# Winograd pairs in the second half of the third projections of a two-block transformer kernel

## What is computed

```python
h = rms_norm(x, norm_g[l])
proj = h @ w_in[l]
(aq, ak, av, az, iq, ik, iw, bcq, bckv, bkpe, bz, cq, cz, gates) = jnp.split(proj, IN_OFFSETS, axis=-1)
...
o_c = memory_attention(cq, ck, cv).reshape(bsz, seq, C_WIDTH)
u = jnp.stack([o_a * jax.nn.silu(az), o_b * jax.nn.silu(bz), o_c * jax.nn.silu(cz)], axis=2)
```

## Time and profile before

| | us |
|---|---|
| median of three runs | 2404.72 |
| the profiled execution | 2404.98 |
| its span, first to last instruction | 2403.2 |
| TensorE busy | 2396.6 |
| VectorE busy | 1852.0 |
| ScalarE busy | 1233.5 |
| GpSimd busy | 321.2 |

### The profile page before, as it was taken

One profiled execution on the slowest core, in us unless ns is written; L12 is line 12 of the kernel. 1 busy time (PEld: TensorE's weight loads), 2 busy tenths in 40 slices (PEclk: granted clock), 3 DMA queues, 4 the chain that ended last, 5 costly groups with the idle time before them and its releaser, 6 DMA issues.

```text
span 2403.2 us, 34102 instructions
## 1 busy us (share of the span) xinstructions
PE 2396.6 (100%) x10809; PEld 1981.8 (82%) x10809; DVE 1852.0 (77%) x2664; ACT 1233.5 (51%) x1582; POOL 321.2 (13%) x277
## 2 busy tenths in 40 slices
PE   9999999999999999999999999999999999999999
PEld 7888888888888888888888888888888888888887
DVE  5467679897888988988888897668867876587584
ACT  5445455555455444444444455455557555555443
POOL 0021242234210000000000000011101000521050
PEclk9999999999999999999999999999999999999999
DMA  7555555576655655555555556955554545544654
GB/s 272 192 186 178 179 178 175 183 245 228 226 186 184 202 197 193 190 194 189 189 199 194 194 190 210 253 185 177 184 190 163 180 166 182 177 167 167 227 193 166
DMA packets 134827, 464.25 MB, mean 193 GB/s; under 512 B 14544, under 2 KB 21328, under 8 KB 134112
## 3 DMA queue, kind: packets, MB, share of 16 engines
q1 hardware_dynamic: 122464, 443.08, 54.4%
q10 hardware_dynamic: 12256, 20.15, 2.7%
q0 software_dynamic: 32, 0.03, 0.0%
HBM read 455.87 MB, written 7.34 MB: 193 GB/s over the span
## 4 chain that ended last, share of the span: by engine, by line
PE 96%; DVE 2%; issue 1%; ACT 1%; DVEq 0%; ACTq 0%
PE PS L682 21%; PE PS L684 21%; PE PS L683 21%; PE PS L931 7%; PE PS L929 7%; PE PS L930 7%; PE PS L949 3%; PE PS L950 3%; PE PS L951 3%; DVE WL L1727 1%; DVE PT L1843 1%; PE PS L798 1%; PE PS L767 1%; PE PS L723 0%; PE PS L1108 0%
## 5 line engine op out<-in xcount | busy, mean ns | idle before, releaser
L1169 ACT ACTIVATE WH<-RAW 128x1024 fp32r<-128x1024 f32 x841 | 888.3, 1059 | 1083.4 <-PE PS L684 684.0
L1727 DVE TENSOR_TENSOR WL<-RAW,WH 128x1024 fp32r<-128x1024 f32 x811 | 1021.0, 1268 | 470.3 <-ACT WH L1169 460.0
L682 PE MATMUL PS<-WH,HT 128*128 128x512 f32 (+1 forms) x1816 | 715.7, 394 | 0.3 <-DVE WL L1727 0.2
L684 PE MATMUL PS<-WH,HT 128*128 128x512 f32 (+1 forms) x1816 | 706.1, 389 | 0.0
L683 PE MATMUL PS<-WL,HT 128*128 128x512 f32 (+1 forms) x1816 | 705.4, 388 | 0.0
L682 PEld LDWEIGHTS PS<-WH,HT 128*128 128x128 f32 x1816 | 341.1, 188 | 71.8 <-issue 3.7
L684 PEld LDWEIGHTS PS<-WH,HT 128*128 128x128 f32 x1816 | 340.9, 188 | 71.0
L683 PEld LDWEIGHTS PS<-WL,HT 128*128 128x128 f32 x1816 | 341.2, 188 | 67.9
L929 PE MATMUL PS<-WH,HT 128*128 128x512 f32 x704 | 274.0, 389 | 0.0
L931 PE MATMUL PS<-WH,HT 128*128 128x512 f32 x704 | 273.9, 389 | 0.0
L930 PE MATMUL PS<-WL,HT 128*128 128x512 f32 x704 | 273.9, 389 | 0.0
(11 more groups left out here) (320 smaller groups left out, 2338.5 us busy)
## 6 DMA issues: line engine op xcount, KB each, us to landing
RAW<-w_stream SPq DMA_DIRECT2D x841, 512.0 KB, 3.4
bias_scratch<-BE ACTq DMA_DIRECT2D x12, 256.0 KB, 4.0
MEMR<-mem_in ACTq DMA_DIRECT2D x1, 2048.0 KB, 10.7
X<-x_in ACTq DMA_DIRECT2D x4, 512.0 KB, 5.1
x_scratch<-X ACTq DMA_DIRECT2D x4, 512.0 KB, 5.1
X<-x_scratch ACTq DMA_DIRECT2D x1, 2048.0 KB, 11.2
out<-X ACTq DMA_DIRECT2D x8, 256.0 KB, 3.1
X<-x_in SPq DMA_DIRECT2D x3, 512.0 KB, 9.3
```

Source lines behind the costliest of these rows:

```text
L682: pe.matmul(o, hi, WH[:, slot, kk, 0:cols], start=k == 0, stop=False)
L684: ins = pe.matmul(o, lo, WH[:, slot, kk, 0:cols], start=False, stop=k == nq * GK - 1)
L1169: act.activation(WH[:, g.slot(j)], RAW[:, g.slot(j)], ACT.Copy).then_inc(hi_split, 1)
L1727: dve.tensor_tensor(WL[:, s], RAW[:, s], WH[:, s].bitcast(F32), ALU.subtract).then_inc(lo_split, 1)
```

## The change

The second half of `c_proj` (groups 16 to 31, product chunks 2 and 3) becomes one product of 2x2 blocks. The rows of `h` split in halves (t = 0, 1), the columns in chunks 2 and 3, and the inner dimension in eight pairs of 128-feature tiles, q = 0 to 7. The stream is read in another order, so that groups 2i and 2i+1 are both chunks for the same q, with q in the order 4, 0, 5, 1, 6, 2, 7, 3.

For q = 0 to 3 (`eight`) the pair is done as before with eight block products. For q = 4 to 7 (`seven`) it is done with Winograd's seven block products M1 to M7. Their left sums S1 to S4 are made once by GpSimd from `HROWS`, which VectorE now scales by the gains at steps 0 to 3; ScalarE and VectorE split them at steps 9 and 10. Their right sums are made for each pair s = 0 to 3 from the group slots a and b: GpSimd makes T3 = B22-B12 into `TX`, then T1 = B12-B11 in place in `RAW` of b, then T2 = B22-T1; VectorE makes B21-T2. ScalarE's split of b waits for T1. ScalarE splits three sums (`TXH`), VectorE their low parts (`TXL`) behind the next group's split. `TX` and its split parts have two buffers. The products run in the order M1, M2, M5, M3, M6, M7, M4; M6 waits for `tx_lo`. The load that takes the slots of a and b waits for `tx_made`. All eight banks hold sums; at the end ScalarE copies one and VectorE adds the parts together into `PB`, seven additions from PSUM, in place of ScalarE's two copies.

```diff
         HROWS = sb("HROWS", [P, KT // 2, S], F32, at_pa + 24 * KB)
+        HBLK = HROWS[:].rearrange("p (q e) (t s) -> p q e t s", e=2, t=T)
+        TX = [sb(f"TX{n}", [P, 3, CH], F32, at) for n, at in enumerate((at_pa, at_pa + 24 * KB))]
+        SUMH = sb("SUMH", [P, 4, 4, P], F32R, at_pa + 8 * KB)
+        SUML = sb("SUML", [P, 4, 4, P], F32R, at_pa + 16 * KB)
+        SUMR = sb("SUMR", [P, 4, 4, P], F32, at_u0)
+        TXH = sb("TXH", [P, 2, 3, CH], F32R, at_x)
+        TXL = sb("TXL", [P, 2, 3, CH], F32R, at_u0)
+        ZU = [sb(f"ZU{n}", [P, CH], F32, at) for n, at in enumerate((at_x + 12 * KB, at_x + 14 * KB, at_pa + 32 * KB, at_pa + 34 * KB))]
         MEMT = sb("MEMT", [P, KT, 2, S], F32R, at_pb)
         MEMX = sb("MEMX", [P, KT, S], F32, at_pa)
         MQKV = sb("MQKV", [P, T, 3 * W], F32, at_pb)
@@ -329,6 +337,18 @@
         x_loaded = sem("x_loaded")
         mem_turned = sem("mem_turned")
...
+        M1, M2, M3, M4, M5, M6, M7, C22 = range(8)
+        own = 2 * (PROD0["c_proj"] % 2)
+        other = 2 - own
+        BANK = {M1: 4, M2: 5, M5: 6, M3: 7, M6: own, M7: own + 1, M4: other, C22: other + 1}
+        HALFWAY = 2 * GD
+        PAIR_Q = (4, 0, 5, 1, 6, 2, 7, 3)
+
+        def seven_of(j):
+
+            i = (j - HALFWAY) // 2
+            return i // 2 if 0 <= i < GD and i % 2 == 0 else None
...
-            with sp.Fori(1, GROUPS // RING) as r:
-                for s in range(RING):
-                    sp.wait_ge(lo_split, r * RING + (s + 1 - RING))
-                    load(None, ds(r * RING + s, 1), s)
+            paired = GROUP0["c_proj"] + HALFWAY
+            assert paired % RING == 0
+
+            def rounds(first, last):
+                with sp.Fori(first // RING, last // RING) as r:
+                    for s in range(RING):
+                        sp.wait_ge(lo_split, r * RING + (s + 1 - RING))
+                        load(None, ds(r * RING + s, 1), s)
+            rounds(RING, paired)
+            for j in range(2 * GD):
+                s = seven_of(HALFWAY + j - RING)
+                if s is not None:
+                    sp.wait_ge(tx_made, s + 1)
+                sp.wait_ge(lo_split, paired + j + 1 - RING)
+                load(None, ds(paired + j % 2 * GD + PAIR_Q[j // 2], 1), j % RING)
+            sp.wait_ge(tx_made, GD // 2)
+            rounds(paired + 2 * GD, GROUPS // RING * RING)
...
+            hold(rows_scaled, 1)
+            a11, a12, a21, a22 = [HBLK[:, :, e, t, :] for t in range(T) for e in range(2)]
+            s1, s2, s3, s4 = [SUMR[:, n] for n in range(4)]
+            link(pool.tensor_tensor(s1, a21, a22, ALU.add))
+            link(pool.tensor_tensor(s2, s1, a11, ALU.subtract))
+            link(pool.tensor_tensor(s3, a11, a21, ALU.subtract))
+            pool.tensor_tensor(s4, a12, s2, ALU.subtract).then_inc(sums_made, 1)
+            hold(sums_made, 1)
+            for s in range(GD // 2):
+                g, j = At(GROUP0["c_proj"]), HALFWAY + 4 * s
+                a, b = g.slot(j), g.slot(j + 1)
+                hold(raw_landed[a], g.turn(j) * 16 + 16)
+                hold(raw_landed[b], g.turn(j + 1) * 16 + 16)
+                if s >= 2:
+                    hold(tx_lo, s - 1)
+                b11, b12, b22 = RAW[:, a, 0], RAW[:, b, 0], RAW[:, b, 1]
+                link(pool.tensor_tensor(TX[s % 2][:, 2], b22, b12, ALU.subtract))
+                pool.tensor_tensor(b12, b12, b11, ALU.subtract).then_inc(t1_made, 1)
+                hold(t1_made, s + 1)
+                pool.tensor_tensor(TX[s % 2][:, 0], b22, b12, ALU.subtract).then_inc(t2_made, 1)
...
             products("c_proj", [(GD, HT)] * 2, 0, None, h3_rest)
-            product_loop("c_proj", 2, [(GD, HT)] * 2, first=1)
+
+            gc, nc0 = At(GROUP0["c_proj"]), PROD0["c_proj"]
+
+            def block_products(o, left, wide, start, stop):
+                (hi, lo), (bh, bl) = left, wide
+                pe.matmul(o, hi, bh, start=start, stop=False)
+                pe.matmul(o, hi, bl, start=False, stop=False)
+                return pe.matmul(o, lo, bh, start=False, stop=stop)
+
+            def tile(k, t):
+                cols = slice(t * P, (t + 1) * P)
+                return HT[:, k, 0, cols], HT[:, k, 1, cols]
+
+            def eight(q, j, first, last):
+
+                for c, outs in enumerate(((M2, M4), (M3, C22))):
+                    def body(slot):
+                        for kk in range(GK):
+                            for t in range(T):
+                                ins = block_products(PS[:, BANK[outs[t]], :], tile(q * GK + kk, t), (WH[:, slot, kk], WL[:, slot, kk]),
+                                                     first and outs[t] == C22 and kk == 0, last and kk == GK - 1)
+                        return ins
+                    group(gc, j + c, body)
+
+            def seven(q, j, s, first, last):
+
+                a, b = gc.slot(j), gc.slot(j + 1)
+
+                def sums(n):
+                    return SUMH[:, n, q - 4, :], SUML[:, n, q - 4, :]
+
+                def wide(slot, kk):
+                    return WH[:, slot, kk], WL[:, slot, kk]
+
+                def extra(n):
+                    return TXH[:, s % 2, n], TXL[:, s % 2, n]
+                k = GK * q
+                parts = {M1: (tile(k, 0), wide(a, 0)), M2: (tile(k + 1, 0), wide(a, 1)), M3: (sums(3), wide(b, 1)),
+                         M4: (tile(k + 1, 1), extra(1)), M5: (sums(0), wide(b, 0)), M6: (sums(1), extra(0)), M7: (sums(2), extra(2))}
+                for m in (M1, M2, M5, M3, M6, M7, M4):
+                    if m == M1:
+                        pe.wait_ge(lo_split, gc.count(j + 1))
+                    if m == M5:
+                        pe.wait_ge(lo_split, gc.count(j + 2))
+                    if m == M6:
+                        pe.wait_ge(tx_lo, s + 1)
+                        if first:
+                            pe.wait_ge(prod_free, nc0 + 3)
+                    if m == M4 and first:
+                        pe.wait_ge(prod_free, nc0 + 4)
+                    ins = block_products(PS[:, BANK[m], :], *parts[m], first, last and m in (M1, M5, M6, M7))
+                    if m in (M2, M3):
+                        ins.then_inc(group_used, 1)
+                    if m == M4:
+                        ins.then_inc(tx_used, 1)
+            pe.wait_ge(sums_lo, 1)
+            for i, q in enumerate(PAIR_Q):
+                j = HALFWAY + 2 * i
+                if i % 2 == 0:
+                    seven(q, j, i // 2, i == 0, i == GD - 2)
+                else:
+                    eight(q, j, i == 1, i == GD - 1)
...
             for p in range(4 * GD):
                 g = At(GROUP0["c_proj"])
+                s = seven_of(p + RING) if p % 2 else None
+                if s is not None:
+                    act.wait_ge(t1_made, s + 1)
                 split(g, p + RING)
                 if p < 3:
                     turned_hi(2, (10 + 2 * p, 11 + 2 * p), "norm2")
-                evacuations("c_proj", g, 0, p, 4, lambda c: PB[:, :, c:c + CH])
+                if p == 9:
+                    act.wait_ge(sums_made, 1)
+                    act.activation(SUMH[:], SUMR[:], ACT.Copy).then_inc(sums_hi, 1)
+                if s is not None:
+                    act.wait_ge(tx_made, s + 1)
+                    if s >= 2:
+                        act.wait_ge(tx_used, s - 1)
+                    act.activation(TXH[:, s % 2], TX[s % 2][:], ACT.Copy).then_inc(tx_hi, 1)
+                if p < HALFWAY:
+                    evacuations("c_proj", g, 0, p, 4, lambda c: PB[:, :, c:c + CH])
+                if p == 4 * GD - 3:
+                    act.wait_ge(tx_used, GD // 2)
+                    act.activation(ZU[0][:], PS[:, BANK[M1], :], ACT.Copy).then_inc(z_copied, 1)
...
+            z, u2, u3, u4 = [part[:] for part in ZU]
+
+            def add(o, m, x):
+                return dve.tensor_tensor(o, PS[:, BANK[m], :], x, ALU.add)
+
+            def c_out(t, c):
+                return PB[:, t, (2 + c) * CH:(3 + c) * CH]
             for p in range(4 * GD):
                 if p < 4:
                     turned_lo("h3", (8 + 2 * p, 9 + 2 * p), "norm2")
+                    for k in (8 + 2 * p, 9 + 2 * p):
+                        o = HROWS[:, k - HALF]
+                        dve.wait_ge(tr_lo, TR["h3"] + k + 1)
+                        ins = dve.tensor_scalar(o, o, par("norm2", k), None, ALU.mult)
+                    if p == 3:
+                        ins.then_inc(rows_scaled, 1)
                 split(At(GROUP0["c_proj"]), p + RING)
+                s = seven_of(p + RING) if p % 2 else None
+                if p == 10:
+                    dve.wait_ge(sums_hi, 1)
+                    dve.tensor_tensor(SUML[:], SUMR[:], SUMH[:].bitcast(F32), ALU.subtract).then_inc(sums_lo, 1)
+                if s is not None:
+                    dve.wait_ge(t2_made, s + 1)
+                    a = At(GROUP0["c_proj"]).slot(p + RING - 1)
```

(26 more changed lines are left out.)

12 lines of the change are left out of this document (added).

## The result

The changed kernel takes 2419.86 us, the median of 2418.0 to 2420.29, beside 2404.76 (2404.53 to 2404.99) for the kernel before: 1.0061 times as long, 95% interval 1.0051 to 1.0071. It is 15.1 us slower where 5.7 were forecast, and lies above the range (2405.0 to 2416.5). The profiled execution took 2419.76.

What follows compares the result with a forecast made beforehand. The prediction took TensorE alone to bound the kernel. Its terms, -2.72 + 4.0 + 4.3 + 0.1 = +5.7 us on the profiled 2404.98, gave 2410.7, or 2410.4 for the median; range 2405.0 to 2416.5.

Steps and rivals of the forecast that it cites:

- Removed: In four c_proj pairs, 21 matmuls in place of 24: 2.72 us saved, all on the bound.
- First pair: TensorE's wait before the first M6 in c_proj: 3.5 us, with 0.5 from upstream 4.0.
- `tx_made` to `tx_lo`: Splitting the right sums on ScalarE, then VectorE's low parts behind the next group's: 5.42 us.
- Landing to `tx_made`: From group b's landing until GpSimd and VectorE have made the right sums: 5.56 us.
- Upstream: VectorE's scalings at steps 1 to 3 and GpSimd's four sums delay loads: 0.5 us, bounds 0 and 2.
- The rings: Later pairs' loops from `tx_made` to `tx_made`: 12.3, 11.3, 11.3 against 10.20 us of TensorE; waits total 4.3 us.
- the latency: Load time of the next a and b: 5.5 us first, 4.5 for the last two; bounds 3.2 and 8.5.
- the meeting: GpSimd's T3 runs beside VectorE's low part of a: 0.75 us more per loop; by the lock 1.4 more in all.
- rival C: Waits near 4 us drop TensorE to the 1.2 GHz level; one return costs 2.2 us: 2412.6; chance 0.15.
- Left sums: ScalarE's and VectorE's splits at steps 9 and 10 lie in leads of over 5 us: nothing.
- The end: Last pair's additions and later Silu use up a_proj's 1.4 us of room: 0.1 us, bounds 0 and 0.5.
- D: Slower parts: GpSimd 1.62 per operation (3.4 us) or first looped load 8.5 (3.0 us); 2413.4 to 2416.8; chance 0.16.

Runs made afterwards that it cites:

- x8: Changed kernel without c_proj's eight bias transfers, bias additions replaced by clears at the start of the next phase's queue; 2412.86 us, ratio 1.0036.
- x2: Changed kernel with T3, T1 and T2 made by VectorE instead of GpSimd, ahead of its low part of b, B21-T2 right behind; 2409.21 us, ratio 1.0021.
- x3: Changed kernel with eighteen extra matmuls, results thrown away, ahead of the first wait before M6; 2422.0 us, ratio 1.0073.
- x7: Changed kernel with only its end mended: bias additions moved to next phase, a_proj's banks freed earlier, Silu and waits reordered; 2417.21 us, ratio 1.0051.
- x0: Changed kernel with M6, M7 and M4 taking split left sums, so TensorE does not wait for `tx_lo`; right sums still made; 2419.51 us, ratio 1.0059.
- x1: Changed kernel with M6, M7 and M4 of the first three pairs put behind the following eight-product pair; 2419.22 us, ratio 1.006.
- x4: Changed kernel without c_proj's eight bias transfers, bias additions replaced by clears in VectorE's steps 26 and 28; 2418.07 us, ratio 1.0055.

## Why the prediction was wrong

The direction and the mechanism were right: late waits before M6 in each pair, ended by `TXL`, and a ring through the loads. The sizes were not, and the clock and the end, which it took as nearly nothing, were not nothing. By its own steps, in us:

- *Removed, 2.72.* Right.
- *First pair, 4.0; it was 4.5.* `tx_made` to `tx_lo`, 5.42, was 5.39. Landing to `tx_made` was 5.96 for 5.56: GpSimd's operation takes 1.28, and half of line 577's 2.41 came out too short (0.17 for the two); VectorE's low part of b took 1.35 for 1.14 beside T2. Upstream was put at 0.5 between 0 and 2. It was 1.0 to 1.1: b landed at 1545.24 for 1544.50, and TensorE was 0.3 earlier. But it did not come the way that I had given, by low parts that delay the load: the load was issued at 1535.55, before at 1535.97, and took 9.6 us for 8.5. What made it longer no run shows. TensorE's restart took back 0.2 (0.06 behind `TXL` for 0.27), and small gaps before M6 another 0.2.
- *The rings, 12.3, 11.3 and 11.3; they were 13.9, 12.7 and 12.7.* This is the step that failed: 4.4 us. The first has the latency 7.5, not 5.5, and no meeting. I had both bounds, and took the lower part although the step before said that two bias transfers would be issued at about the same moment. x8 without them gives 12.7, with the meeting. The others have the meeting: I charged 0.75, one operation of GpSimd against one of VectorE. But VectorE comes to it late, with three low parts back to back, so T1 and T2 meet it too: 7.8 for 5.9 from landing to `tx_made`, 1.9 a ring. Without the meeting these two rings would be 10.8 by the same rows, an estimate. x2, where nothing meets and the sums take 2.9, has 10.45, and there VectorE's queue sets it.
- *The clock (rival C, 0.15).* It happened twice, at 2.5 and 1.7 where one return was priced at 2.2. That it has a rival's name and not a place in the sum is a second miss. What I had missed: a fall inside a ring that binds is free (x3), so the length of the wait is not what prices it, but whether anything behind it can take it up. The one behind the last wait cost 1.7 (nine matmuls in 3.75 us for 2.04).
- *Left sums, nothing.* No wait of TensorE is theirs. Their first operation took 4.38, beside four low parts that took 5.73; whether that has a part in the late landing above is not tested, since no run leaves them out.
- *The end, 0.1, bounds 0 and 0.5; it was 1.8* (2.61 for 0.77 behind c_proj). I had seen that the room of 1.4 us was used up by a Silu 1.4 later, and then charged 0.1. Silu came 4.8 after the last group for the forecast's 3.7, behind pair additions that were late themselves, with two bias additions (1.75 each) ahead of them on VectorE. A spent room is not a price of nothing but one from which every further delay counts in full. x7 takes 1.0 of it; the 0.8 at the head values stays.
- *Overlooked.* The evacuation of chunk 1 stands behind ScalarE's wait for `tx_made`, and its bank is M4's. It costs nothing while M6 is later, but it alone would have kept 1.9 of the wait (x0), and 3.3 of it where TensorE comes earlier (x1).

Together 0.5 + 4.4 + 1.7 + 1.7 = 8.3, of the 14.3 - 5.7 = 8.6 that the profiled span is longer than forecast. The rest is small.

The range failed for a reason of its own: D took one slower part at a time, C one fall by itself. In the trace the falls stood behind waits that the long ring made, and the end was late with the fourth pair, so they came together.

On the meeting, the third pair's rows say this: from 1570.04 to 1577.20, 7.16 us, VectorE did three low parts and GpSimd its three operations, which take 3.5 and 3.86 when they are alone, 7.36 in all. The two engines hardly overlapped. The ends of the six operations alternate: GpSimd's at 1571.65, 1573.88 and 1576.12, VectorE's, each asked for by itself, at 1572.73, 1574.97 and 1577.20. Each comes 1.1 us behind the one before, as if one worked while the other stood. The Trainium skill, page "SBUF — State Buffer", section "SBUF: two separate sides", says that an exclusive lock for a whole instruction governs this pair of engines; the trace agrees here (7.16 of 7.36), and in the left sums, where GpSimd's 4.38 is 1.28 and the better part of three low parts of 1.14. The prediction had named the lock, but charged it for T3 alone and took the smaller loss of one row, 0.75, in its place.

## What to carry to other kernels

When new work is put between a load and the release of its slot, add up the whole ring (release, issue, latency, each engine's part) and hold it against the time that the consumer needs for one turn; if it is longer, the consumer's waits inside it, their order and its clock are not worth mending (x0, x1, x3), only the ring is. When a ring is shortened, look for the next one: in x2 it was VectorE's queue. Operations like those of this kernel, each reading two tensors of SBUF, that run on VectorE and GpSimd at the same time are to be summed, not laid beside each other: here four subtractions on VectorE alone (2.9 us) beat three on GpSimd and one on VectorE (5.9 to 7.8). Where a gain is a few matmuls, look also at what is queued behind the new waits at the end of the stage, and take the late cases of a range together when they have one cause.

## What the runs showed of the hardware

- A 128x512 subtraction from SBUF takes GpSimd 1.28 us and VectorE 0.69. Where VectorE's low parts run beside it, GpSimd's takes 1.6 to 2.06, once 4.38, and the profile shows it as a longer operation, not as idle time. The low part is longer too, 2.2 to 2.3 for 1.22.
- Behind waits of TensorE of 3.27 to 4.34 us (changed, x1, x3, x4, x7) the granted clock was 0.50 to 0.52 for about 5 us each time. Behind shorter ones it fell in some (1.89 in x0, 2.69 in x1, 2.15 before the changed kernel's fourth M6, 2.20 in x8's second, there from 1.4 us after the wait) and stayed at 1.00 in others (the third of the changed kernel, the fourth of x7 and of x8, 2.19 to 2.20). What divides them is open. The Trainium skill, page "TensorE: Matmul & The Clock Gate", section "Part 1: The HAM clock gate", says that the clock is set by how busy TensorE has been recently; these rows don't contradict it, since the length of one wait doesn't decide, but they don't show it either.
- The profile page's row of granted clock shows 9 in all its slices even so: a fall of 5 us is lost in a slice of 60, and is found by the spacing of starts or by a window.
